# Modulation vectors summed as rows, later lows earlier, and one norm between two halves: a two-layer transformer in float32 on one core

## What is computed

```
shift, scale, gate = split(silu(c) @ ada_w[layer, i] + ada_b[layer, i]);  gate = 1 + gate
h = x * (1 + scale) + shift
y = mixer(h)                  # i = 0: window and sparse attention (layer 0), causal attention (layer 1)
y = square(relu(h @ w1)) @ w2 # i = 1
x = layer_norm(DN_ALPHA * x + gate * y, ln_g[layer, i], ln_b[layer, i])
```

```
q = rms_norm(q, q_norm_g);  k = rms_norm(k, k_norm_g)   # full attention, per head of 64
o = softmax(rope(q) @ rope(k).T / 8) @ v
x = x + (o * silu(gate)) @ w_out
```

## Time and profile before

| | |
|---|---|
| median of 3 runs | 1054.5 us (1053.75 to 1055.5) |
| the profiled execution | 1052.61 us, its span 1050.8 us |
| TensorE busy | 978.2 us, 93% of the span |
| VectorE busy | 720.1 us, 69% |
| ScalarE busy | 543.6 us, 52% |
| granted clock of TensorE, mean | 0.980 |
| DMA | 204.85 MB, mean 195 GB/s |

### The profile page before, as it was taken

How to read it: one execution, slowest core, us unless ns; L and a number is a source line. 1 busy time by engine, 2 the same in 40 slices (tenths; PEclk the granted TensorE clock), 3 DMA queues, 4 the chain that set the end, 5 groups by cost and what they waited for, 6 DMA issues and landing times.

```text
span 1050.8 us, 14669 instructions
## 1 busy us (share of the span) xinstructions
PE 978.2 (93%) x5692; PEld 792.5 (75%) x5692; DVE 720.1 (69%) x1113; ACT 543.6 (52%) x869; POOL 49.2 (5%) x39
## 2 busy tenths in 40 slices
PE   6886998999999989999899999989999999998995
PEld 2663666989898866777699989877788887875684
DVE  3488668777776587565885554478654778797775
ACT  3367725544453253555355455435565746656662
POOL 0000003200000000000071100000000000000000
PEclk9999999999999989999999999999999999999998
DMA  9747476879897468332689776554434346551041
GB/s 350 245 145 295 161 240 214 287 258 341 298 328 261 160 238 294 127 118 64 200 269 254 209 234 188 183 190 132 149 121 130 121 141 200 187 174 61 32 160 40
DMA packets 106931, 204.85 MB, mean 195 GB/s; under 512 B 3488, under 2 KB 37680, under 8 KB 106864
## 3 DMA queue, kind: packets, MB, share of 16 engines
q1 hardware_dynamic: 103808, 193.25, 54.8%
q0 software_dynamic: 3056, 10.67, 3.5%
HBM read 202.76 MB, written 1.15 MB: 194 GB/s over the span
## 4 chain that ended last, share of the span: by engine, by line
PE 66%; DVE 17%; ACT 7%; DMA 6%; issue 3%; SPq 1%; ACTq 0%; DVEq 0%
PE bank L1672 13%; PE bank L1674 13%; PE bank L1673 13%; DVE w_lo L1851 5%; PE bank L1726 5%; PE bank L1728 4%; PE bank L1727 4%; DMA raw<-in_mlp_w 3%; PE bank L1747 2%; ACT w_hi L1293 2%; PE bank L1769 2%; DMA raw<-in_ada_w 2%; DMA raw<-in_ab_w_in 1%; PE bank L1574 1%; PE bank L1814 1%
## 5 line engine op out<-in xcount | busy, mean ns | idle before, releaser
L1851 DVE TENSOR_TENSOR w_lo<-raw,w_hi 128x2048 fp32r<-128x2048 f32 (+2 forms) x134 | 308.6, 2311 | 154.5 <-ACT w_hi L1293 153.4
L1293 ACT ACTIVATE w_hi<-raw 128x2048 fp32r<-128x2048 f32 (+2 forms) x134 | 248.5, 1857 | 131.3 <-PE bank L1674 69.2
L1672 PE MATMUL bank<-w_lo,ht_hi 128*128 128x512 f32 (+1 forms) x544 | 218.4, 401 | 12.5 <-DVE w_lo L1851 7.8
L1674 PE MATMUL bank<-w_hi,ht_lo 128*128 128x512 f32 (+1 forms) x528 | 206.4, 391 | 0.0
L1673 PE MATMUL bank<-w_hi,ht_hi 128*128 128x512 f32 (+1 forms) x528 | 206.1, 390 | 0.0
L1672 PEld LDWEIGHTS bank<-w_lo,ht_hi 128*128 128x128 f32 x544 | 103.7, 191 | 41.8 <-issue 21.4
L1726 PE MATMUL bank<-ht_hi,w_lo 128*128 128x256 f32 x448 | 127.5, 285 | 2.4 <-DVE w_lo L1851 2.4
L1727 PE MATMUL bank<-ht_lo,w_hi 128*128 128x256 f32 x448 | 126.8, 283 | 0.0
L1728 PE MATMUL bank<-ht_hi,w_hi 128*128 128x256 f32 x448 | 126.8, 283 | 0.0
L1674 PEld LDWEIGHTS bank<-w_hi,ht_lo 128*128 128x128 f32 x528 | 100.5, 190 | 21.3
L1673 PEld LDWEIGHTS bank<-w_hi,ht_hi 128*128 128x128 f32 x528 | 101.0, 191 | 18.8
(11 more groups left out here) (244 smaller groups left out, 1334.2 us busy)
## 6 DMA issues: line engine op xcount, KB each, us to landing
raw<-in_mlp_w SPq DMA_DIRECT2D x64, 1024.0 KB, 6.0
raw<-in_ada_w SPq DMA_DIRECT2D x44, 1024.0 KB, 5.3
raw<-in_a_w_in SPq DMA_DIRECT2D x16, 1024.0 KB, 5.3
raw<-in_c_w_in SPq DMA_DIRECT2D x12, 1024.0 KB, 5.4
raw<-in_b_w_in SPq DMA_DIRECT2D x10, 1024.0 KB, 5.1
raw<-in_ple_w_gate SPq DMA_DIRECT2D x8, 1024.0 KB, 5.0
raw<-in_ab_w_in SPq DMA_DIRECT2D x4, 1024.0 KB, 9.8
tok<-in_ada_w SPq DMA_DIRECT2D x4, 1024.0 KB, 12.8
```

Source lines behind the costliest of these rows:

```text
L1293: nc.scalar.activation(split_parts(n)[0], raw_tile(t), ACT.Copy).then_inc(high_done, 1)
L1672: nc.tensor.matmul(dst, a_hi[:, c, rows], lo[:, k, :], start=it["first"] and k == 0, stop=False)
L1674: mm = nc.tensor.matmul(dst, a_lo[:, c, rows], hi[:, k, :], start=False, stop=it["last"] and k == it["kc"] - 1)
L1851: nc.vector.tensor_tensor(lo, raw_tile(split[n]), hi.bitcast(F32), ALU.subtract).then_inc(low_done, 1)
```

## The change

It has six parts.

1. A new item `sum_rows`: for a part that stands in sums, TensorE adds the 128 partitions with 32 equal columns of ones as weights, 256 columns moving, into four groups of 32 rows (4 matmul calls, one for each quarter of the 1024 columns). ScalarE copies the 128 x 256 back over the sums. `columns` then takes four columns at a time with a constant `quads`, 2 calls in place of 8. For s = 2 both stand in `down(2)` now, for s = 3 in `down(3)`: `sum_rows` after the first weight tile of the left half, `columns` after the second.
2. `down(3)`: `ahead_by` 3 for both left tiles (was 3 and 2) and 3 and 2 for the parted ones (was 2 and 1).
3. `last_tiles` (both attentions of the first block): 3 and 2 ahead at the first two items (was 2 and 1); `columns(1, 1)` stands between them, where it was ahead of `last_tiles` before.
4. End of both attentions: one more tile ahead at the left items of the output matrix; for the first attention the gate row comes after the left half of the second token tile.
5. `halves`: the norm of the second token tile stands between the two pieces of the first tile's turn.
6. `q_scale` stands ahead of the third pair's minima, and a gate tile's low part one step later.

The diff:

```diff
 _at = 0
-for _name, _n in (("ident", P), ("ones", 1), ("sel", 2), ("four", 1), ("axcos", T * HD), ("axsin", T * HD), ("near", GRID),
+for _name, _n in (("ident", P), ("ones", 1), ("sel", 2), ("four", 1), ("quads", 4), ("axcos", T * HD), ("axsin", T * HD), ("near", GRID),
                   ("causal", P), ("window", P), ("invf", HD), ("sign", HD)):
...
     put("four", np.isin(np.arange(P), (0, 32, 64, 96))[:, None])
+    put("quads", np.stack([np.arange(P) == 32 * g for g in range(4)], 1))
     put("causal", np.where(col <= row, 0.0, -MASKED))
...
 
+    def sum_rows(s, part, bank):
+
+        it = add("sum_rows", s=s, part=part, after=ada_end[s, part][1], banks=banks((bank,)), job=tick("job"))
+        ada_end[s, part] = ("quads", evicted(it))
+
     def columns(s, part, pairs=None):
...
                         continue
-                    it = add("tokens", tile=t, kc=4, width=512, lhs=("hid", g % 2), off=h * 4, banks=yb[n], ts=(0, 1), ahead_by=3 - h if g == 3 else None,
+                    it = add("tokens", tile=t, kc=4, width=512, lhs=("hid", g % 2), off=h * 4, banks=yb[n], ts=(0, 1), ahead_by=3 if g == 3 else None,
                              first=g == 0 and h == 0, last=g == 3 and h == 1, cut=hid_cut[g], enter=g == 0 and h == 0, half=tick("half"))
...
                         ada_tiles(1)
-                    if g == 3 and h == 0 and layer == 0:
-                        columns(3, 0)
-                        columns(3, 1)
+                    if g == 3 and layer == 0:
+                        for part in range(2):
+                            if h == 0:
+                                sum_rows(3, part, part)
+                            else:
+                                columns(3, part, (2 + part,))
+                    if g == 2 and layer == 0 and n == 0:
+                        for part in range(2):
+                            if h == 0:
+                                sum_rows(2, part, part)
+                            else:
+                                columns(2, part, (2 + part,))
                 if g == 3 and n == 0:
...
                     it = add("tokens", tile=parted[h][0], kc=4, width=512, lhs=("hid", 1), off=h * 4, banks=yb[1], ts=(t,),
-                             first=False, last=h == 1, cut=hid_cut[3], enter=False, ahead_by=2 - h)
+                             first=False, last=h == 1, cut=hid_cut[3], enter=False, ahead_by=3 - h)
                     if t == 0:
...
             down(0, each), up(2, (1, 3)), down(1, each), up(3, (1, 3))
-            columns(2, 0)
-            columns(2, 1)
             down(2, (0, 2)), down(3)
...
 
-    def across(s, t, places, engines):
+    def across(s, t, places, engines, between=None):
 
         for half in range(2):
+            if half and between:
+                between()
             it = add("turn_rows", s=s, t=t, a=4 * half, banks=banks((places[half],)), job=tick("job"), wait=rows_of[s - 1, t]["rows"],
...
 
-        y[0](1, 2, ts=(0,))
-        y[1](1, 1, ts=(0,), spare=True)
+        y[0](1, 3, ts=(0,))
+        if s == 0:
+            columns(1, 1, (7,))
+        y[1](1, 2, ts=(0,), spare=True)
         norm_ln(s, 0)
...
 
-        across(s, 0, (0, 1), ("act", "act"))
+        across(s, 0, (0, 1), ("act", "act"), lambda: norm_ln(s - 1, 1))
         if extra:
             ada_tiles(2, 7)
-        norm_ln(s - 1, 1)
         first(0, 1, ts=(0,), cut=cuts["ht", 0][0])
...
     o_last = values(7)
-    y[1](0, 1, ts=(0,), look=4)
+    y[1](0, 2, ts=(0,), look=4)
     split_out(1, o_last)
     ada_tiles(2)
+    y[1](0, 3, ts=(1,))
     gate_row(0, (6, 7))
-    columns(1, 1, (7,))
-    y[1](0, 2, ts=(1,))
     last_tiles(0)
...
     scores(7, [turned[7]]), values(5), probs(6)
-    y[0](0, 1, ts=(1,))
+    y[0](0, 2, ts=(1,))
     values(6), probs(7)
-    y[1](0, 1, ts=(0,), look=4)
+    y[1](0, 2, ts=(0,), look=4)
     o_last = values(7)
+    add("next_high", until=count["split"] + 2)
     split_out(1, o_last)
-    y[1](0, 2, ts=(1,))
+    y[1](0, 3, ts=(1,))
     last_tiles(2)
...
     scores(1, []), probs(0)
-    g[1](1, 1, ts=(0,))
-    scores(2, [turned[2]]), values(0, (kv,)), probs(1)
     add("q_scale")
+    g[1](1, 0, ts=(0,))
+    scores(2, [turned[2]]), values(0, (kv,)), probs(1)
     gates = g[1](1, 1, ts=(1,))
...
 
-    ordered = [i for i in plan if i["kind"] not in ("ada_sum", "ada_product", "ada_rows", "affine", "columns")]
+    ordered = [i for i in plan if i["kind"] not in ("ada_sum", "ada_product", "ada_rows", "affine", "columns", "sum_rows")]
     for it, after in zip(ordered, ordered[1:]):
...
 
+                elif kind == "sum_rows":
+                    b, _ = it["banks"][0]
+                    act.wait_ge(job_done, it["job"])
+                    nc.scalar.activation(sums_of(it)[:, 0:256], bank[b][:, 0:256], ACT.Copy).then_inc(bank_free[b], 1)
+
                 elif kind == "turn" and it["engine"] == "act":
...
 
+                elif kind == "sum_rows":
+
+                    enter(it["banks"])
+                    b = it["banks"][0][0]
+                    pe.wait_ge(sums_done, it["after"])
+                    for g in range(4):
+                        mm = nc.tensor.matmul(bank[b][32 * g:32 * (g + 1), 0:256], const("ones").broadcast_to([P, 32]),
+                                              sums_of(it)[:, 256 * g:256 * (g + 1)], start=True, stop=True)
+                    mm.then_inc(job_done, 1)
+
                 elif kind == "columns":
...
                     part = it["part"]
-                    if it["how"] == "sums":
-                        pe.wait_ge(sums_done, it["after"])
-                        for j in range(KD):
-                            mm = nc.tensor.matmul(bank[b][:, j:j + 1], sums_of(it)[:, j * P:(j + 1) * P], const("ones"),
+                    enter(it["after"])
+                    if it["how"] == "quads":
+                        for i in range(2):
+                            mm = nc.tensor.matmul(bank[b][:, 4 * i:4 * i + 4], sums_of(it)[:, i * P:(i + 1) * P], const("quads"),
                                                   start=True, stop=True)
                     else:
-                        enter(it["after"])
                         for i in range(4):
...
                         src = src.rearrange("p (i c) -> p i c", c=2)
+                    elif it["how"] == "quads":
+                        dst, bias = (v.rearrange("p (g i) -> p i g", g=4) for v in (dst, bias))
+                        src = src.rearrange("p (i g) -> p i g", g=4)
                     nc.vector.tensor_tensor(dst, src, bias, ALU.add).then_inc(bank_free[b], 1)
...
                         dve.wait_ge(job_done, it["job"])
+                        if it["emptied"]:
+                            dve.wait_ge(split_done, it["emptied"])
                         for c in range(4):
```

More of the change, by code:

```diff
@@ L871, in make_plan @@
     scores(1, []), probs(0)
-    g[1](1, 1, ts=(0,))
+    add("q_scale")
+    g[1](1, 0, ts=(0,))
     scores(2, [turned[2]]), values(0, (kv,)), probs(1)
-    add("q_scale")
     gates = g[1](1, 1, ts=(1,))
```

## The result

| | before | changed |
|---|---|---|
| median of 4 runs | 1054.12 us (1053.19 to 1055.5) | 1038.22 us (1036.38 to 1041.39) |
| ratio, 95% interval | | 0.9869 [0.984, 0.9899] |
| the profiled execution, its span | 1052.61, 1050.8 us | 1036.38, 1034.6 us |
| TensorE busy | 978.2 us | 967.8 us |
| granted clock, mean | 0.980 | 0.986 |

The change gained 15.9 us in the median (1054.12 - 1038.22), where 11.6 was forecast. The four runs of the kernel before lie high: 78 later runs of it, taken beside the experiments, have the median 1052.65, and against them the gain is 14.4.

The account below looks back on a forecast made before the run. TensorE, busy 978.2 of 1050.8 us, was taken as the bound, leaving idle time and tiny or half-clock matmuls to win. The terms summed to -11.6 us, from 1054.5 to 1042.9 us, range 1040.4 to 1049.8.

Parts of the forecast that it names:

- Columns by rows: Two runs of 16 one-column calls near 314 and 347 us become fewer, shorter matmuls: -3.1 us.
- The clock behind the columns: Half-clock dips right behind the two runs of one-column calls disappear: -3.4 us, 1.7 each.
- Rival B: The half-clock dips behind the columns stay, since small matmuls remain: 1046.3 us; this or the border's clock rival alone, chance 0.25.
- One more low part before the norms: End of the first MLP: an added low part ahead of eviction L2109 on VectorE costs +0.7 us.
- Rival D: Added low part ahead of L2109 uncovered, norms and transposes 2.8 us later at all four borders: 1057.2 us, chance 0.06.
- Border after the first MLP: Entry into second attention: earlier norm -1.9, earlier low part -0.4, clock holds -3.4; together -5.7 us.
- Border before the second MLP: Wait for the first ht_lo stays; output-matrix matmuls wait a little less for low parts: -0.5 us.
- Border before the first MLP: Spare tile's low part delays norm and transposes 2.8 us, mostly caught up: +1.0 us, between -1 and +3.
- Second queries' root: Chain near 960 us moves into VectorE's idle time, cutting a TensorE wait of 1.48: -0.6 us, 0 to -2.
- Border after the second MLP: Norm's move leaves the idle time of 2.66 us, VectorE sets the pace: 0, at best -2 us.
- Rival A: Low clock at the border after the first MLP stays or moves within it: 1046.3 us; this or columns' rival alone, 0.25.
- Rivals C and E: First: low parts bind in first MLP, half the gain, 1048.5 us, chance 0.08; second: no effect, 1054 us, chance 0.05.

Follow-up runs that it names:

- t1: Kernel before, its one-column calls spread as 8 after each of four weight tiles instead of 16 in a row twice; median 1049.12 us, ratio 0.9966.
- e1_rows_only: Kernel before plus only the row sums (`sum_rows`, `quads`, new places of `columns`); median 1047.17 us, ratio 0.9968.
- e2: Kernel before plus only the earlier norm of the second token tile in `halves`; median 1052.01 us, ratio 0.9997.
- f6: Changed kernel with the look ahead in `down(3)` put back as before; median 1044.22 us, ratio 0.9913.
- f2: Changed kernel with the second token tile's norm put back behind both pieces of the turn; median 1040.28 us, ratio 0.9909.
- f1: Changed kernel without the row sums, one-column calls back at their old places; median 1044.73 us, ratio 0.9933.
- f4: Kernel before plus the earlier low parts, later gate row and earlier norm, without row sums or `q_scale` move; median 1045.98 us, ratio 0.9941.
- e3: Kernel before plus only the low parts of weights one tile earlier and the gate row later; median 1050.94 us, ratio 1.0003.
- e4: Kernel before plus only the `q_scale` move and the gate tile's later low part; median 1054.28 us, ratio 1.0013.
- second trace: The changed kernel run once more, unaltered, for another trace and more times; median 1037.76 us, ratio 0.9876 against the kernel before.
- f5: Changed kernel without the `q_scale` move and the gate tile's later low part; median 1037.39 us, ratio 0.9857.
- f3: Changed kernel with the end of the first attention in its old order, gate row and columns first; median 1036.81 us, ratio 0.9837.

## Why the prediction fell short

Point by point, by its own steps:

- **Columns by rows, -3.1:** right; 2.9 by t1. The Trainium skill (TensorEngine Tiling (Array Packing), Key Properties) warns of a drain of TensorE when the tiling mode changes. An entry costs 0.1 us here (0.32 from 320.32 to 320.64, where two matmuls stand 0.23 apart), as the sum had it, and no more shows.
- **The clock behind the columns, -3.4:** right against this trace (3.0), and caused by the packs, as t1 shows: 16 calls in a row bring it, 8 don't. Rival B fell. In the five other kernels with the packs it is 5.1, which the one trace of before did not show.
- **One more low part before the norms, +0.7:** wrong. The stage from 311 to 369 us comes out at -6.0 with it and, in e1_rows_only, without it. At the end of the first MLP the first eviction stands right behind the added low part (350.18), but the third is back at its bank's end (357.89 against 357.79), and TensorE waits no longer for the norm. Rival D, which wanted +2.8 at every border, fell with it. Its mechanism is real at one border: at the end of the first attention the eviction came 2.7 us behind its bank, and this the forecast had priced on its own.
- **Border after the first MLP, -5.7:** right in size (-5.4), wrong in its parts, and so in part by luck. The norm's move gave its 2.0 of idle time. But the clock, which I laid to the end of that idle time alone, does not hold without item 2: the step that I priced at -0.4, "made one place earlier by item 2, is ready", decides it. Without item 2 a wait of 1.86 takes the place of the 2.11, with half clock behind it (e2, f6). With items 2 to 4 in place the clock held where item 1 or item 5 stood beside them (f2; f1 and f4), and not where neither did (e3); why is open. The wait of 1.86 is the sign of being wrong that the prediction had named, a wait for w_lo over 1 us in place of the gap. I read the price of the low part from its present wait of 0.39, though the norm's move would uncover it.
- **Second attention, put at nothing without a reason:** -1.2 in both traces. Once the entry runs at full speed, the wait of 1.13 us for a transfer of `ada_w` at 404 us is gone. All seven traces without half clock behind the entry show this; the six others of changed kernels (e1 to e4, f6, t1) do not. In all of them TensorE wants the tile some 6.6 us behind its issue, if nothing holds it; the transfer lands 5.0 to 6.3 us after its issue in the seven, and 7.7 to 9.1 after it in the others and in the kernel before. Why it takes longer there was not tried.
- **Border before the second MLP, -0.5:** mis-sized, -1.4. The wait for the norm fell from 1.20 to 0.71 (0.75 in the second trace), and the half clock of 1.7 behind the next wait is gone, though that wait stayed (2.17 before, 2.13 and 2.17 now). Of the traces with items 3 and 4 five lack it (both of the change, f1, f5, f6) and four have it (e3, f2, f3, f4), so the 0.7 that parts the two groups (-1.4 against -0.7) may be chance.
- **Border before the first MLP, +1.0:** right (+0.65 and +0.5). The transposes come 2.4 later (2.8 forecast), 1.8 come back, and the wait of 0.75 at the hidden matmuls fell to 0.22. f3_no_4a was to take it away, and its trace does not show that (+0.65).
- **Second queries' root, -0.6:** right in its stage (-0.7 and -0.9); that it shortens the whole is not shown (e4, f5).
- **Border after the second MLP, 0 and at best -2:** -1.8 and -0.1, the first with less low clock. Most of this is chance between executions: of the thirteen traces, the seven with 1.7 us of low clock in this stage stand at -0.5 to -1.8, the six with 3.4, as in the kernel before, at -0.6 to +0.2. Among the seven, the four with item 5 are 0.7 to 1.3 shorter than the three without it, so the move may be worth something here too; no run shows it alone.
- **The first 137 us, not in the sum:** -0.9, though the change doesn't touch their order. A half-clock stretch lies at 28 us in some traces and at 43 us in others, in kernels of either kind, and with equal low clock up to 137 us the traces with the first are 1.3 to 1.8 us shorter. This is chance.

Added up, the rows with a forecast (entry into the first MLP, second matrix, both entries after it, root) came to -12.8 and -13.2 where -11.6 was forecast. The second attention adds -1.2, and the rows of chance -2.2 in the first trace and -1.1 in the second. So of the 4.6 us between the forecast and the first trace, 1.2 lie in mis-sized terms (most of it the second MLP's border, -1.4 for -0.5), 1.2 in the second attention, and 2.2 are luck.

The step that failed is the price of item 2: a cost of +0.7 with a return of 0.4 in the prediction, where the cost was nothing and the change without it is 6.5 us slower. In the sum this was mostly hidden, since I had laid the 3.4 of the clock to the norm alone; what came out beyond the sum is the second attention, whose wait comes back without item 2 (+2.45 in f6, -1.2 in the change). Rival A, the low clock that stays at the entry, is what item 5 without item 2 gives. Rivals C and E have nothing in the traces for them. And the low end of the range had no room for low clock that is absent by chance, though a single execution of either kernel varies by several us through it.

## What to carry to other kernels

A wait that an edit removes is worth what is late next, and the price of that next thing must be read for the new time, not from its present wait: here the norm's move and the earlier low part gave 0.4 and 1.5 us alone and 6.6 together. The tiny matmuls of this kernel cost 0.10 to 0.12 us each, with one, two or four columns, and those of 256 columns into 32-row groups 0.06; so it paid to sum into rows first, and where tiny ones must stay, 8 calls in a row did better than 16. And look at what stands in front of ready work on an engine: the spare tile's low part here held CAST, whose inputs were ready, behind a wait of 4.87 us. What that cost in the end is not shown.

## What the runs showed of the hardware

- Half clock came behind 32 tiny matmuls (16 calls) that had kept TensorE busy without a pause, in all six traces that have such packs (the kernel before, e2, e3, e4, f1, f4), and behind none of the places in the eight where they stand by eights or are replaced. The Trainium skill (TensorE: Matmul & The Clock Gate, HAM oscillation) tells of idle gaps between bursts; here full use of the engine by small matmuls did the same. Why is not shown.
- An idle time is no sure cause either: 2.11 us before the transposes was followed by half clock in the kernel before and 2.13 in e3, while 2.14 at the same place in f2_no_norm was not.
- Each half-clock stretch inside a trace lost 1.7 or 3.4 us, and their number and place vary between executions of one kernel: 17 to 35 runs of the kernel before on one chip range over 8 to 11 us.
